# Norms of the attention items: 256-token statistics groups and inverse roots spread as high and low parts

## The reference, cut to what matters

```
def rms_norm(x, gain):
    xf = x.astype(jnp.float32)
    y = xf * lax.rsqrt(jnp.mean(xf * xf, axis=-1, keepdims=True) + EPS)
    return (y * gain.astype(jnp.float32)).astype(x.dtype)

q = (rms_norm(cq, q_norm) @ w_uq).reshape(b, t, MLA_HEADS, MLA_NOPE + MLA_ROPE)
q = mla_qk_norm(q, q_gain)                  # rms_norm of the first 128, and of the last 64
q = concatenate([q[..., :128], axial_rotary(q[..., 128:], angs)])
kv = (rms_norm(ckv, kv_norm) @ w_ukv).reshape(b, t, MLA_HEADS, MLA_NOPE + MLA_V)
k_nope = rms_norm(kv[..., :128], k_gain[:128])
k_rope = rms_norm(k_rope, k_gain[128:])     # one for all heads, then rotary
```

## Time and profile before

| | |
|---|---|
| median of three runs | 3266.49 us |
| the profiled execution | 3265.89 us, its span 3264.2 us |
| TensorE busy | 3095.1 us, 95% of the span |
| VectorE, ScalarE busy | 56%, 27% |
| chain that ended last | 89% TensorE, 6% VectorE, 3% ScalarE |
| mean granted TensorE clock | 0.982 of full speed |

### The profile page before, as it was taken

One profiled execution on the slowest core, in us unless ns is written; L12 is line 12 of the kernel. 1 busy time (PEld: TensorE's weight loads), 2 busy tenths in 40 slices (PEclk: granted clock), 3 DMA queues, 4 the chain that ended last, 5 costly groups with the idle time before them and its releaser, 6 DMA issues.

```text
span 3264.2 us, 42549 instructions
## 1 busy us (share of the span) xinstructions
PE 3095.1 (95%) x17560; PEld 2655.0 (81%) x17560; DVE 1833.8 (56%) x2670; ACT 866.4 (27%) x1188; POOL 36.7 (1%) x73
## 2 busy tenths in 40 slices
PE   6999999879999999999999999999799999989999
PEld 4888888767777788888888888888678787778887
DVE  4765565645655576655664455567454636464444
ACT  3211111433443431111132111113222223242221
POOL 0000000000000000000000000000000000000000
PEclk8999999989999999999999999999899999999999
DMA  6333232110111043323221232231111111122222
GB/s 236 131 130 112 90 116 90 46 39 27 51 39 39 27 155 116 116 99 107 103 90 55 75 116 103 90 116 54 62 56 51 67 47 65 43 74 97 96 91 89
DMA packets 40977, 277.72 MB, mean 85 GB/s; under 512 B 4352, under 2 KB 5632, under 8 KB 8000
## 3 DMA queue, kind: packets, MB, share of 16 engines
q1 hardware_dynamic: 31024, 205.85, 17.9%
q0 software_dynamic: 9872, 70.72, 6.1%
HBM read 274.45 MB, written 2.10 MB: 85 GB/s over the span
## 4 chain that ended last, share of the span: by engine, by line
PE 89%; DVE 6%; ACT 3%; issue 1%; DMA 1%; SPq 0%; DVEq 0%; POOL 0%; ACTq 0%
PE ps L299 29%; PE ps L301 28%; PE ps L300 28%; PE ps L613 2%; PE ps L327 1%; DVE wl L1212 1%; ACT wh L856 1%; DVE act_buf L1296 1%; DVE xnl L1300 1%; PE ps L313 0%; DMA ada_w<-ada 0%; DVE nrm L1507 0%; ACT xnh L887 0%; PE ps L345 0%; PE ps L412 0%
## 5 line engine op out<-in xcount | busy, mean ns | idle before, releaser
L299 PE MATMUL ps<-xnh,wl 128*128 128x512 f32 (+1 forms) x3040 | 1063.4, 350 | 35.6 <-DVE wl L1212 14.8
L300 PE MATMUL ps<-xnl,wh 128*128 128x512 f32 (+1 forms) x3040 | 1053.9, 347 | 0.0
L301 PE MATMUL ps<-xnh,wh 128*128 128x512 f32 (+1 forms) x3040 | 1052.8, 346 | 0.0
L299 PEld LDWEIGHTS ps<-xnh,wl 128*128 128x128 f32 x3040 | 582.3, 192 | 118.1 <-DVE xnl L1300 16.5
L301 PEld LDWEIGHTS ps<-xnh,wh 128*128 128x128 f32 x3040 | 582.4, 192 | 70.0
L300 PEld LDWEIGHTS ps<-xnl,wh 128*128 128x128 f32 x3040 | 582.8, 192 | 68.1 <-issue 1.0
L856 ACT ACTIVATE wh<-raw 128x2048 fp32r<-128x2048 f32 (+1 forms) x178 | 332.7, 1871 | 607.1 <-PE ps L301 607.1
L1212 DVE TENSOR_TENSOR wl<-raw,wh 128x2048 fp32r<-128x2048 f32 (+1 forms) x183 | 410.2, 2242 | 112.8 <-ACT wh L856 112.6
L1354 DVE SCALAR_TENSOR_TENSOR h<-ps,coef,h 128x512 f32<-128x512 f32 x624 | 371.9, 642 | 129.9 <-PE ps L301 129.5
L301 PE MATMUL ps<-hidh,wh 128*128 128x512 f32 (+1 forms) x1232 | 429.3, 348 | 0.0
L299 PE MATMUL ps<-hidh,wl 128*128 128x512 f32 (+1 forms) x1232 | 425.7, 346 | 3.1 <-DVE h L1312 3.1
(11 more groups left out here) (226 smaller groups left out, 3090.4 us busy)
## 6 DMA issues: line engine op xcount, KB each, us to landing
raw<-weights SPq DMA_DIRECT2D x183, 1024.0 KB, 4.8
adaw<-ada POOLq DMA_DIRECT2D x64, 1024.0 KB, 5.1
ada_w<-ada SPq DMA_DIRECT2D x8, 1024.0 KB, 20.4
h<-x_in SPq DMA_DIRECT2D x1, 2048.0 KB, 9.0
c_act<-c_rows POOLq DMA_DIRECT2D x2, 1024.0 KB, 5.1
out<-h SPq DMA_DIRECT2D x8, 256.0 KB, 2.0
h<-x_in SPq DMA_DIRECT2D x1, 1024.0 KB, 28.3
cs<-rope_mla POOLq DMA_DIRECT2D x1, 512.0 KB, 3.4
```

The source lines that it names most:

```text
L299: mm(dst, lhs[1][rows], rhs[0][rows], start=first, stop=False)
L300: mm(dst, lhs[0][rows], rhs[1][rows], start=False, stop=False)
L301: return mm(dst, lhs[0][rows], rhs[0][rows], start=False, stop=last)
```

## The change

The statistics of an item now lie as three groups of 256 tokens on 3 x 32 = 96 partitions by 256 columns. `item_sum` issues three ones-products of 256 columns. `root` and the reciprocal of `inverse` work on 96 x 256. `inverse` then also makes a high part (a copy to f32r) and a low part (a subtraction) of the inverse roots, in memory that is free at that time (`qn` in the once-only part, the attention output's `oo`, a slice of `xnh` and `xnl`, in the pairs); each of the two waits for the instruction before it. A full spread is six f32r products of 256 columns, low and high part for each group, against a column of `sel`, an f32r copy of `quarter` made once by ScalarE. The halved spread of item 0 still reads `irms` in fp32: six products of 64 output partitions by 256 columns, the two halves alternating, but it waits for the same semaphore, which now comes after the low part.

```diff
-        irms = sb("irms", [P, T // 4], F32, mla_mem)
+        irms = sb("irms", [P, L], F32, mla_mem)
+        sel = sb("sel", [P, 8], F32R, mla_mem)
...
+        def irms_parts(pre):
+            if pre:
+                return qn[0:96, 0, 0, 0:L], qn[0:96, 1, 0, 0:L]
+            return oo[0][0:96, 0, 0:L], oo[1][0:96, 0, 0:L]
...
             def item_sum(bank, at=L, first=True, last=True, mat=ones):
                 pe.wait_ge(item_sq, c.next(item_sq))
-                quarter_sums(bank, at, sqb, T, first, last, mat).then_inc(item_ms, 1)
-
-            def item_spread(halves=1):
+                for g in range(3):
+                    ins = mm(ps[32 * g:32 * g + 32, bank, at:at + L], mat, sqb[:, g * L:g * L + L], start=first, stop=last)
+                ins.then_inc(item_ms, 1)
+
+            def item_spread(halves=1, pre=False):
 
                 pe.wait_ge(item_inv, c.next(item_inv))
-                spread((6, 7), irms[:], T, halves).then_inc(item_rms, 1)
+                if pre:
+                    pe.wait_ge(sel_ready, 1)
+                part_hi, part_lo = irms_parts(pre)
+                for g in range(3):
+                    bank, col = ((6, 0), (6, L), (7, 0))[g]
+                    if halves == 2:
+                        for i in range(2):
+                            ins = mm(ps[64 * i:64 * i + 64, bank, col:col + L],
+                                     quarter[0:96, 2 * g + i:2 * g + i + 1].to_broadcast([96, 64]), irms[0:96], start=True, stop=True)
+                        continue
+                    pick_g = sel[0:96, 2 * g:2 * g + 1].to_broadcast([96, P])
+                    mm(ps[:, bank, col:col + L], pick_g, part_lo, start=True, stop=False)
+                    ins = mm(ps[:, bank, col:col + L], pick_g, part_hi, start=False, stop=True)
+                ins.then_inc(item_rms, 1)
...
-                fn(irms[:], ps[:, bank, at:at + T // 4], ACT.Sqrt, bias=eps[:, 0:1], scale=1.0 / dim
+                fn(irms[0:96], ps[0:96, bank, at:at + L], ACT.Sqrt, bias=eps[0:96, 0:1], scale=1.0 / dim
                    ).then_inc(item_std, 1)
...
+            fn(sel[:], quarter, ACT.Copy).then_inc(sel_ready, 1)
...
-            def inverse():
+            def inverse(pre=False):
+                part_hi, part_lo = irms_parts(pre)
                 dve.wait_ge(item_std, c.next(item_std))
-                nc.vector.reciprocal(irms[:], irms[:]).then_inc(item_inv, 1)
+                nc.vector.reciprocal(irms[0:96], irms[0:96]).then_inc(item_half, 1)
+                dve.wait_ge(item_half, c.next(item_half))
+                nc.vector.tensor_copy(part_hi, irms[0:96]).then_inc(item_half, 1)
+                dve.wait_ge(item_half, c.next(item_half))
+                tt(part_lo, irms[0:96], part_hi.bitcast(F32), ALU.subtract).then_inc(item_inv, 1)
```

More of the change, by code:

```diff
@@ L207, in build @@
         item_inv, item_rms = sem("item_inv"), sem("item_rms")
+        item_half, sel_ready = sem("item_half"), sem("sel_ready")
         item_v, item_swapped, item_rot = sem("item_v"), sem("item_swapped"), sem("item_rot")
@@ L571, in _ @@
             item_sum(6, 0, False, True)
-            item_spread()
+            item_spread(pre=True)
             project(3, w_in(s1, 1), xn, KD)
@@ L1522, in _ @@
             split_lo(s0)
-            inverse()
+            inverse(pre=True)
             g = gate_cols["q_norm"]
@@ L1628, in pair @@
                 split_lo(s1)
-            with c.loop(dve, PAIRS - 1, {item_std: 5, item_hi: 5, item_swapped: 1, v_hi: 3, s_full: 12, exp_done: 12,
+            with c.loop(dve, PAIRS - 1, {item_std: 5, item_half: 10, item_hi: 5, item_swapped: 1, v_hi: 3, s_full: 12, exp_done: 12,
                                          pt_hi: 12, o_hi: 4, y_full: 16, w_hi[0]: 2, w_hi[1]: 2, item_rms: 5,
```

## The result

The kernel after takes 3293.02 us (median of four runs, 3290.16 to 3298.41), the kernel before 3266.16 in runs made beside it: ratio 1.0084, interval 1.0067 to 1.0102. The forecast was 3278 us, 12 slower, with a range of 3270 to 3286. Slower was right, but by 27 us and not by 12, and the time lies above the range. The profiled execution after took 3298.41 us, 32.5 more than the profiled one before, so the trace has to account for 32.5.

What follows compares the result with a forecast made beforehand. In layer 0's norms, VectorE's queue and the chain of spread, scaled and reciprocal were taken to set the pace. 3265.89 + 10.4 (four pairs) + 1.1 (once-only) = 3277.4, with 0.6 for the median 3278 us; range 3270 to 3286.

Steps and rivals of the forecast that it cites:

- The inverse, +1.17 us: VectorE, each of 23 inverses: wider reciprocal +0.40, cast 0.29, subtraction 0.42, two waiting steps 0.06.
- The spreads: TensorE: a full spread as six f32r products takes 0.91 us (-0.60), the halved one about 1.45 (-0.93).
- The cast to f32r: VectorE, in each inverse: 0.29 us for 256 columns, estimated from an SBUF copy, bounds 0.15 and 0.42.
- The walk, +2.6 per pair: Norms of each head pair, lateness followed item by item: a pair is 2.6 us longer, four pairs +10.4.
- Item 0's longer sum is covered as taken: Start of each pair: ScalarE's square-root table load hides item 0's longer sum; if not, +0.1 more.
- The line that sums the walk up: Per pair: 5.85 added on VectorE, 0.93 + 2 x 0.6 given back by spreads, about 2.1 covered, leaving 2.6 us.
- Its waits of "about 1.5 us": Sign to look for: TensorE waits about 1.5 us for the reciprocal's low part before spreads 2 and 3.
- the 0.6 before the first scores: Sign to look for: a new TensorE wait of 0.6 us before the first scores of a pair.
- The once-only part, +1.1: Norms ahead of the pairs: first spread +0.45, two later sums +0.2, second and third norm together +0.5.
- The softmax loops as long as before: Loops behind the norms: they start later as a whole, with unchanged length, and absorb none of the delay.
- rival 3: The clock: TensorE's new waits, about 1.5 us each before spreads 1, 2 and 3, lie close together; chance 15%.
- the 3286 of the range: Slow end of the forecast: a slow cast, halves one after the other, and part of a clock loss.

Runs made afterwards that it cites:

- the alternating halves alone: Kernel before with only the product order of the halved spread changed, so that its two halves of 64 output partitions alternate: 3266.28 us, ratio 0.9994.
- the first filler run: Kernel after plus 8, 10 and 12 unused f32r products on TensorE ahead of its waits for spreads 1, 2 and 3 of every pair: 3299.0 us, ratio 1.008.
- all waits filled: Kernel after plus unused f32r products ahead of spreads 1, 2, 3 and 4, the first scores and the first `turn`: 3280.77 us, ratio 1.004.
- the run with the head filler: Kernel after plus four unused f32r products ahead of each of spread 4, the first scores and the first `turn`: 3283.44 us, ratio 1.0048.
- the kernel with the three memsets: Kernel before plus three VectorE memsets of 768 columns (0.70 us each) at the head of each pair's softmax loop: 3299.13 us, ratio 1.01.
- the run with the groups alone: Kernel after without high and low parts: 96 x 256 reciprocals, full spreads as three fp32 products: 3267.61 us, ratio 0.9999.
- the last two versions: Kernel before with alternating halves, six fillers before the swap, third once-only inverse ahead of a weight split: 3266.04 us; the same plus 44 once-only fillers: 3263.72 us.

## Why the prediction was right in direction and too small

- The inverse, +1.17 us: right. Cast 0.289 and subtraction 0.422 to the hundredth, 2.44 us from reciprocal to the next instruction where 1.27 stood before (third pair, behind inverse 2).
- The spreads, 0.91 for the full and 1.45 for the halved one: right to 0.01. That the two halves would run side by side was an estimate from the four strips of a sum (0.46 us); the alternating halves alone show it, 1.45 us for 2.38. A broadcast column in f32r loads like others: in 188 ns (median of L566 with `xnh`, after), where broadcast fp32 columns take 190 (median of L327 before) and other weights of 128 x 128 take 192 (mean of L299 before).
- The cast to f32r ran at about the pace of the plain copy that its 0.29 was worked out from: 64 columns more cost it 289 - 260 = 29 ns, where the copy's 427 ns less 153 for 512 columns give an estimate of 34 for 64. The subtraction's 64 columns more cost 422 - 358 = 64 ns.
- The walk, +2.6 per pair: right in its steps, too long in its size. The trace has +2.6 from the swap to the first `turn` (23.55 for 20.97), but the walk counted from the pair's start, with the swap already 0.3 early, so it had +2.9 there. Item 0's longer sum is covered as taken: ScalarE's table load ahead of its root takes 1.28 us at 842.90, and the root starts at its end, 844.20 (second pair of after). The swap comes 0.4 to 0.6 us early (from the last `turn` 38.36 us in the first filler run for 38.75, 39.69 with all waits filled for 40.31), and from loop to loop a pair costs 2.0 to 2.1 us: 8 us in four pairs for the 10.4. The line that sums the walk up does not come out either: 5.85 less 0.93, 1.2 and 2.1 is 1.6, and for 2.6 only 1.1 could be covered.
- Its waits of "about 1.5 us" were 1.45 and 1.63 before spreads 2 and 3, and 0.45 for the 0.6 before the first scores.
- The once-only part, +1.1: the trace has +2.9 on 78.11 us. The low clock around its third spread lasted 27.3 us for 20.5, and 6.8 for 3.4 at the first spread. I had taken that clock as it was. This term too small and the pairs too large nearly cancel: that the run with all waits filled came out at 3280.8 us, near the 3278, is in part luck.
- "The softmax loops as long as before": wrong, and this is the step that failed. It is the case of rival 3, which I gave 15%. I priced it at 1.7 us for each pair, 6.8 in all, and the 3286 of the range holds a part of that. The price was my estimate from the earlier trace rows, where the clock fell behind the gap between two pairs: a mean of 0.64 over 4.7 us is 3.4 us at half speed, and half of those are lost. No run shows this price for the new waits: I took one duration of such a fall for the only one. At the head of the softmax loop it stayed for 23.9 and 13.7 us, and cost 10.5 and 6.0. I also named the wrong waits: those of 1.2 to 1.6 us before spreads 1 to 3 did not decide the loops (open in the run with the head filler, all four loops at full clock; filled in the first filler run, three of four lost time), the three of half a microsecond did, which stand directly ahead of the loop.

The trace held a warning that I did not read: in the once-only part of the kernel before one stretch at half speed lasts 20.5 us, at 691.5 us. Part of it is waiting (9.11 us ahead of the third spread end in it), so it does not show how long a fall lasts in busy time. But as an upper end it would have given a fall a price of some 10 us, an estimate from 20.5 us at half speed, and with two such falls the range would have reached past 3293.

So the sum by mechanism, in the profiled execution, is: norms 11.4 with 1.0 of low clock in them, less 0.5 ahead of the swaps, together 10.9 for the predicted 10.4; once-only 2.9 for 1.1; loops 16.5 for 0; 2.3 ahead of the first sum and behind the last loop for 0. By the medians the loops are about 12 (3293.0 less the 3280.8 of the run with all waits filled, which was made on another chip).

## What to carry to other kernels

Before adding work to an engine that feeds TensorE, look where the new waits of TensorE fall: here 1.44 us in three small ones directly ahead of a long dense phase cost 10.5 us in one pair and 6.0 in another, and four filler matmuls in each (0.48 us) gave that back. Price a clock fall by the longest stretch at the low level that the trace of the same program holds, not by the commonest. And a cheaper matmul gains only where the pace-setting engine waits for it: the f32r spreads are 0.55 us shorter each than fp32 ones of 256 columns, 2.2 us per pair, of which 1 us reached the norms (24.56 against 23.6), and the rest became waits.

## What was not expected of the hardware

- Once down at the head of the loop, the clock stayed at half speed (0.50) for 23.9 us although TensorE was busy for every one of them, then 13.7 us in the second pair; the kernel with the three memsets has the same two figures, 13.7 in its third and 3.4 in its fourth. Why the lengths differ from pair to pair with the same instructions stays open.
- Two fp32 product streams of 64 output partitions each, alternating, take no longer than one stream of 128: 12 records of 256 columns in 1.45 us, where a full fp32 spread of 6 such records takes 1.46 (the run with the groups alone).
- Executions of one kernel differ by 7 to 9 us (3261.8 to 3268.9 and 3259.6 to 3268.5 in the last two versions, whose loops all take 47.6 to 47.7 us in their traces). Each kernel has one trace, so what differs between its executions is not shown; between the traces of near kernels it is stretches of 3.4 or 6.8 us at half speed that come and go.
